# Neighbourhood attention: the bias of the scores added on TensorE, by products with the identity, in the place of VectorE

## The reference, cut to what matters

```
s_n = jnp.einsum('bhqd,bhqnd->bhqn', qblk, kg, preferred_element_type=jnp.float32) + rpb_flat[:, rb].astype(jnp.float32)
s_c = jnp.einsum('bhqd,bhcd->bhqc', qblk, k_c, preferred_element_type=jnp.float32)
p = jax.nn.softmax(jnp.concatenate([s_n, s_c], axis=-1), axis=-1).astype(v_l.dtype)
return jnp.einsum('bhqn,bhqnd->bhqd', p[..., :nk], vg) + jnp.einsum('bhqc,bhcd->bhqd', p[..., nk:], v_c)
```

## Time and profile before

| | us |
|---|---|
| median of 3 runs | 2999.63 |
| lowest and highest | 2997.81, 3007.0 |
| the profiled execution, whole | 2997.95 |
| its span in the trace | 2996.0 |
| PE busy (share of span) | 2883.8 (96%) |
| DVE busy | 1025.0 (34%) |
| ACT busy | 562.4 (19%) |

### The profile page before, as it was taken

How to read it: one execution, slowest core, us unless ns; L and a number is a source line. 1 busy time by engine, 2 the same in 40 slices (tenths; PEclk the granted TensorE clock), 3 DMA queues, 4 the chain that set the end, 5 groups by cost and what they waited for, 6 DMA issues and landing times. The chain is left out here.

```text
span 2996.0 us, 34497 instructions
## 1 busy us (share of the span) xinstructions
PE 2883.8 (96%) x14167; PEld 1664.3 (56%) x14167; DVE 1025.0 (34%) x2664; ACT 562.4 (19%) x1302; POOL 179.0 (6%) x300
## 2 busy tenths in 40 slices
PE   7999999999999999999999999999978989999998
PEld 4576547864468555884556555454434455444443
DVE  3444523421444532541435432222222064222222
ACT  1322411100231421211155110000011051000000
POOL 0000041000000000000000010000012021000000
PEclk9999999999999999999999999999989999999999
DMA  5457647354256545543040379999984227999996
GB/s 213 141 177 252 225 137 249 121 182 145 86 176 243 210 163 202 204 150 108 23 155 5 146 293 428 428 428 427 428 354 149 82 64 275 410 428 427 427 428 266
DMA packets 183445, 708.18 MB, mean 236 GB/s; under 512 B 16563, under 2 KB 25859, under 8 KB 156017
## 3 DMA queue, kind: packets, MB, share of 16 engines
q1 hardware_dynamic: 166624, 668.56, 57.2%
q0 software_dynamic: 16368, 37.32, 3.8%
q10 hardware_dynamic: 288, 0.01, 0.0%
HBM read 700.37 MB, written 11.76 MB: 238 GB/s over the span
## 5 line engine op out<-in xcount | busy, mean ns | idle before, releaser
L643 PE MATMUL bank<-h1T,wslot 128*128 128x256 f32 x2176 | 473.7, 380 | 2.2 <-issue 2.2
L643 PEld LDWEIGHTS bank<-h1T,wslot 128*128 128x128 f32 x2176 | 412.1, 190 | 61.4 <-issue 6.0
L2713 PE MATMUL bank<-wslot,xgT 128*64 128x512 f32 x672 | 296.7, 596 | 6.8 <-DMA another<-in_moe_w_up 2.6
L2730 DVE TENSOR_TENSOR hid<-gs,bank 64x512 f32<-64x512 f32 x65 | 68.6, 1056 | 467.4 <-ACT gs L2724 467.4
L2714 PE MATMUL bank<-wslot,xgT 128*64 128x512 f32 x512 | 226.0, 594 | 0.0
L2685 PEld LDWEIGHTS bank<-sel,hT 128*128 128x128 f32 x1600 | 182.9, 193 | 23.7 <-issue 23.5
L2685 PE MATMUL bank<-sel,hT 128*128 128x128 f32 x1600 | 188.8, 278 | 0.0
L2724 ACT ACTIVATE gs<-bank 64x512 f32<-64x512 f32 x65 | 38.4, 591 | 580.1 <-PE bank L2714 580.1
L2713 PEld LDWEIGHTS bank<-wslot,xgT 128*64 128x64 f32 x672 | 90.7, 137 | 97.8 <-issue 97.8
L506 PE MATMUL bank<-wslot,hT 128*128 128x512 f32 (+3 forms) x320 | 110.1, 498 | 9.0 <-DVE hT L2060 4.1
L2805 PE MATMUL bank<-wslot,aT 128*64 128x512 f32 x336 | 113.3, 595 | 0.0
(11 more groups left out here) (461 smaller groups left out, 4118.8 us busy)
## 6 DMA issues: line engine op xcount, KB each, us to landing
wslot<-in_moe_w_gate SPq DMA_DIRECT2D x41, 2048.0 KB, 18.9
wslot<-in_moe_w_down SPq DMA_DIRECT2D x38, 2048.0 KB, 19.8
wslot<-in_w_in SPq DMA_DIRECT2D x36, 2048.0 KB, 9.3
wslot<-in_moe_w_up SPq DMA_DIRECT2D x32, 2048.0 KB, 15.2
wslot<-in_w_ada SPq DMA_DIRECT2D x24, 2048.0 KB, 8.7
wslot<-in_ffn_w_up SPq DMA_DIRECT2D x20, 2048.0 KB, 8.9
late<-in_moe_w_gate SPq DMA_DIRECT2D x13, 2048.0 KB, 18.7
extra<-in_moe_w_up SPq DMA_DIRECT2D x13, 2048.0 KB, 15.8
```

Of the source, the lines that this page charges most:

```text
L643: ins = pe.matmul(b.t[:, 0:width], w[:, k, j * P:(j + 1) * P], xT(k), start=(k == 0), stop=(k == kc - 1))
L2713: pe.matmul(bk.t[other, :], xt.t[:, k, mine], wg[:, j, :], start=(k == 0), stop=(k == KD - 1))
L2730: K.mv = K.dve.mark(v.tensor_tensor(a_.t[mine, :].rearrange("p (k q) -> p q k", k=DE // P), g_.t[mine, :].rearrange("p (q k) -> p q k", k= ...
```

## The change

In `attend_pair`, where a bias is given, the scores' products no longer close the accumulation in the bank; two further products, the 128 x 128 identity by a head's 128 x 256 bias tile, add it to the latent half of each bank. DVE's addition and the wait behind it go. The wait for `biased` moves from DVE (ahead of the add) to PE (ahead of the scores). `pair` frees the bias table with PE's mark after the scores, one round earlier than it did, and calls `fetch(n + 2)` there. The other calls of `attend_pair` give no bias and are unchanged.

```
-            for due in self.due(pe, *deps, *[m for b in scores for m in b.free]):
+            for due in self.due(pe, *deps, *biased, *[m for b in scores for m in b.free]):
                 pe.wait_ge(*due)
             for i in range(2):
-                ins = pe.matmul(of[i], q[i], k[i], start=True, stop=True)
+                ins = pe.matmul(of[i], q[i], k[i], start=True, stop=bias is None)
+            if bias is not None:
+                for i in range(2):
+                    ins = pe.matmul(of[i][:, first:nk], self.ident, bias[i], start=False, stop=True)
...
-                for due in self.due(v, ready, *stfree, *deps, *biased):
+                for due in self.due(v, ready, *stfree, *deps):
                     v.wait_ge(*due)
-                if bias is not None:
-                    for due in self.due(v, self.dve.mark(v.tensor_tensor(of[i][:, first:nk], of[i][:, first:nk], bias[i], ALU.add)
-                                                         .then_inc(self.dve.sem, 1))):
-                        v.wait_ge(*due)
...
             next(job)
-            yield
-            next(job)
             if t == TT - 1 and j % 2 == 1:
-                b.free = [(K.dve, K.dve.count)]
+                b.free = [(K.pe, K.pe.count)]
                 if n + 2 < HC // 4:
                     fetch(n + 2)
             yield
```

## The result

The changed kernel takes 3016.57 us in the median of nine runs (3012.66 to 3028.73); the kernel before, nine runs beside it, 3001.78 (2997.81 to 3007.0). The ratio is 1.0061 with a 95% interval of 1.0049 to 1.0073, so 15 to 22 us slower; 14.8 by the medians. The forecast was 3014 in a range of 3004 to 3022, slower. The profiled execution took 3016.31 us (span 3014.3) against 2997.95 (span 2996.0): 18.4 us more where the medians differ by 14.8, as the profiled execution of the kernel before was 3.8 us faster than its median.

What follows compares the result with a forecast made beforehand. It took a DVE-ACT loop to hold most attention rounds, with PE the bound afterwards. Terms +3.7 + 1.7 - 0.8 + 9.4 + 1.6 = +15.6 us on 2997.95 gave 3014, range 3004 to 3022.

Steps and rivals of the forecast that it cites:

- twelve rounds, without stalls: Neighbourhood attention, first to thirteenth S: 12 rounds at 4.36 us, 52.3 against 48.6, +3.7 us.
- front: Before the first S: products of pairs 2 and 3 stand ahead of it, +1.7 us.
- tail: From the thirteenth S to the output projection: the last pair's two adds leave the chain, -0.8 us.
- two waits for the windows: PE ahead of the scores of pairs 8 and 12: stalls until DVE adds the windows, 2 x 4.70 = +9.4 us.
- clock: PE's granted clock falls to half after one of the two stalls, +1.6 us; range 0 to 3.2.
- The round of 4.36: A full PE round in the attention: 3.49 us of present work plus 0.87 for a pair's products.
- the 3.49: PE's work per round before the change, read from S at 2446.36 to S at 2449.85 as free of waits.
- Rival C: Products on PE with open weight loads cost 1.52 us a pair, not 0.87: +9.1 more, 3023; chance 0.09.
- A: The window wait costs PE little because DVE has the windows ready: only +4.6 us, 3003; chance 0.11.
- B: Products fit PE's spare 0.56 us a round and the shorter DVE-ACT loop pays: down to 2990; chance 0.03.
- D: The expert stage behind makes up for the delay, so the end doesn't shift: 2998 to 3000; chance 0.05.
- Transfers of the tables: Bias table fetches, called a round earlier and waiting for PE's scores, stay hidden: 0 us.

Runs made afterwards that it cites:

- kernel without additions: The kernel before with the bias left out of the scores, neither added on DVE nor by products on PE: 2988.38 us, ratio 0.9961.
- early-windows run: The changed kernel with the windows of head groups 2 and 3 added on DVE one round earlier: 3005.18 us, ratio 1.0008.
- doubled products: The changed kernel with windows added one round earlier and each bias product issued twice: 3015.82 us, ratio 1.0048.
- wait-only kernel: The kernel before, DVE still adding the bias, with PE also waiting for the window additions ahead of the scores: 3011.2 us, ratio 1.0028.

## Why the prediction was right, point by point

| term | predicted us | measured in the trace |
|---|---|---|
| twelve rounds, without stalls | +3.7 (4.36 each) | +4.0 (12 x 4.385 = 52.6) |
| front | +1.7 | +2.1 (9.66 instead of 7.53) |
| tail | -0.8 | -1.2 (10.92 instead of 12.09) |
| two waits for the windows | +9.4 (4.70 each) | +8.9 (4.44 each) |
| clock | +1.6 (one fall) | +3.3 (two falls) |
| sum | +15.6 | +17.1; the stage is 17.3 longer |

In plain rounds the scores start 0.07 us ahead of T's last result (2433.30 against 2432.28 + 1.09). Behind a stall they don't, and that is most of the 0.2 between the last two numbers. The front holds two pairs' products at 1.06 us. The tail of 10.92 is that of the kernel without additions too, so its gain is theirs.

*The moved wait* was the largest term, rightly placed and sized; the early-windows run shows it from the other side. The error of 0.26 each is in the two maxima, which run closer together when nothing stands between them: from the start of the first to the windows 1.19 us (2438.47 to 2439.66), not 1.45.

*The round of 4.36* is right to 0.03 by luck, through two errors that cancel. The step that took the earlier trace rows for a round in which PE never waits was wrong: without the additions PE's round is 3.32, so 0.17 of the 3.49 was waiting that the view doesn't mark. The kernel before had shown it: its first round, from the S at 2414.56 to this one, is 3.33.

```profile
2417.89 0.44 PE L934 MATMUL bank<-const,stat 128*64 128x128 f32 x4
```

And the products cost 4.39 - 3.32 = 1.07 a pair, not 0.87: a stretch of products brings 0.20 with it, however long it is (0.63 for one, 1.06 for two, 0.87 for two more). Rival C had named a change of shape as its doubt, and this is a third of its price; its ground, open weight loads for every product, is refuted by the doubled products.

*The clock* fell behind both stalls; I had taken one, and this term is the one that was mis-sized. The price of a fall, 1.6 us, was met: 3.76 - 2.12 = 1.64. That is partly luck as well, for it was read from another stretch, and the price isn't fixed: behind the two stalls of the wait-only kernel it was 2.9 and 1.8. The Trainium skill, TensorE: Matmul & The Clock Gate, Part 1, has idle bring the half clock; the trace agrees, 0.50 at 2443.

That 3014 lies within 3 us of the median owes something to chance too: the sum is 1.7 us short of the stage's growth, and the medians lie 14.8 us apart where the profiled executions lie 18.4 apart.

*Rivals.* A is out (4.4 us each, not under 2). B: the loop does pay when nothing is added to PE, by 9.95 us of the stage, and with the early windows the product at 1.07 a pair stands well above the spare time (0.73 against the true 3.32), so the net is a loss. D is out: 520.6 us behind the stage.

*Transfers of the tables* stayed hidden: issued from 2418.49 and 2436.03, and no wait on them in DVE's or PE's list.

## What to carry to other kernels

An engine that is idle 20% of a stage may be idle because it runs ahead; ask what its own round takes with no wait in it before giving it work, and look for an engine with more room: here ACT. When an operation moves to another engine its waits move too, and a wait at the head of an in-order queue stops all that stands behind it; read what the awaited mark is queued behind on its own engine. If a stall on PE can't be moved, its length is not its price: add the half clock behind it, and take off what the rounds behind it have to spare.

## What the hardware showed that I had not expected

A stretch of products 128 deep put between the scores (64 deep, packed in pairs) and S costs about 0.20 us beside its records; a second product in it costs only its 0.43. The records of one stretch in the early-windows kernel show where the 0.20 lies:

```profile
2425.54 0.48 PE L877 MATMUL bank<-late,const 128*128 128x256 f32 x1
2425.86 0.38 PE L877 MATMUL bank<-late,const 128*128 128x256 f32 x1
...
2426.30 0.38 PE L877 MATMUL bank<-late,const 128*128 128x256 f32 x1
2426.60 0.33 PE L933 MATMUL bank<-const,stat 128*64 128x128 f32 x2
```

From the first record to the second it is 0.32 us, and from the fourth and last to S 0.30, where the others stand 0.22 apart: about 0.1 more on entering and 0.1 more on leaving. It isn't the depth alone, for S is 128 deep too and in the kernel without additions stands 1.06 us behind the start of the scores, as the first product does here. What causes it was not tried.

The clock does not fall by the length of a gap alone: the wait of 2.36 us ahead of the third pair's scores left them at 1.13 us in the kernel before, while in one execution of the wait-only kernel the same wait, of 2.36 us as well, was followed by 2.08, at a granted clock of 0.50 (window 2415 to 2416; 1.00 from 2411 to 2413 in the kernel before).

```profile
2411.38 1.13 PE L874 MATMUL bank<-knT,qnT 64*128 64x512 f32 x4 [2.36 <-ACT prob L898]
```

```profile
2414.64 2.08 PE L874 MATMUL bank<-knT,qnT 64*128 64x512 f32 x4 [2.36 <-ACT prob L898]
```

That may be part of why the changed kernel's nine runs spread over 16 us where those of before spread over 9: its mean granted clock is 0.992 in the fastest (3012.66) and 0.987 in the slowest (3028.73). In which stage the slow ones lose it is not known, since they weren't profiled.
